# The projections of a differential-attention layer on one Trainium2 core: seven half-size block products over all 16 k-tiles instead of over 8, with weight sums made by accumulating transfers

## What is computed

```python
proj = u @ w_in                         # 512x2048 @ 2048x8192: q | k | v | z
logits = q_h @ k_h.T * scale + rel_bias # causal, 16 heads of width 128
p = softmax(logits)                     # heads 2i and 2i+1 make one pair
a = p[:, :, 0] - lam * p[:, :, 1]
o = rms_norm(a @ v_pair, subln_g) * (1 - lam_init)
y = (o * silu(z)) @ w_out               # 512x2048 @ 2048x2048
h = layer_norm(alpha * u + y, g, b)
```

## Time and profile before

| | |
|---|---|
| median of 3 runs | 921.08 us (920.71 to 921.26) |
| profiled execution, span from first to last instruction | 918.4 us |
| around the span (median less span) | 2.7 us |
| PE busy | 912.0 us, 99% of the span |
| DVE busy | 609.1 us, 66% |
| ACT busy | 381.8 us, 42% |
| POOL busy | 178.6 us, 19% |
| DMA | 124.53 MB, 136 GB/s on average |
| granted TensorE clock | 1.000 |

### The profile page before, as it was taken

How to read it: one execution, slowest core, us unless ns; L and a number is a source line. 1 busy time by engine, 2 the same in 40 slices (tenths; PEclk the granted TensorE clock), 3 DMA queues, 4 the chain that set the end, 5 groups by cost and what they waited for, 6 DMA issues and landing times.

```text
span 918.4 us, 14283 instructions
## 1 busy us (share of the span) xinstructions
PE 912.0 (99%) x5210; PEld 807.3 (88%) x5210; DVE 609.1 (66%) x1020; ACT 381.8 (42%) x653; POOL 178.6 (19%) x364
## 2 busy tenths in 40 slices
PE   9999999999999999999999999999999999999997
PEld 8888989898989898989898989898989888888886
DVE  5675857675767676767676767576757797434465
ACT  4443544444534354535453535353535454213211
POOL 1300313031303130313031303230322000000033
PEclk9999999999999999999999999999999999999999
DMA  8722506260625062606260625061606424443433
GB/s 308 288 94 97 181 32 198 85 188 23 206 74 188 25 204 78 193 26 197 90 190 26 200 80 188 23 206 46 189 26 217 191 92 160 183 149 99 154 116 114
DMA packets 43274, 124.53 MB, mean 136 GB/s; under 512 B 8160, under 2 KB 10208, under 8 KB 42992
## 3 DMA queue, kind: packets, MB, share of 16 engines
q1 hardware_dynamic: 29328, 97.27, 32.0%
q0 software_dynamic: 9504, 17.75, 6.2%
q10 hardware_dynamic: 4416, 9.18, 2.7%
HBM read 108.01 MB, written 13.15 MB: 132 GB/s over the span
## 4 chain that ended last, share of the span: by engine, by line
PE 99%; DMA 0%; DVE 0%; issue 0%; ACT 0%; SPq 0%; DVEq 0%; ACTq 0%
PE proj L1409 79%; PE att L1409 20%; DMA w_raw<-w_in_tiles_dram 0%; DVE big L1401 0%; DVE last_stats L1387 0%; ACT bias L900 0%; SPq L434 0%; DVE w_split L1250 0%; DVE mean_var L1390 0%; DVEq L1389 0%; ACTq L899 0%
## 5 line engine op out<-in xcount | busy, mean ns | idle before, releaser
L1409 PE MATMUL proj<-w_split,xg_split 128*128 128x512 f32 (+1 forms) x1512 | 294.5, 354 | 0.0
L1409 PEld LDWEIGHTS proj<-w_split,xg_split 128*128 128x128 f32 x1512 | 250.5, 189 | 39.9 <-issue 0.3
L1409 PE MATMUL proj<-xg_split,w_split 128*128 128x512 f32 (+1 forms) x1032 | 203.6, 355 | 0.3 <-DVE w_split L1250 0.3
L1409 PEld LDWEIGHTS proj<-xg_split,w_split 128*128 128x128 f32 x1032 | 171.8, 189 | 27.7 <-ACT xg_split L819 0.5
L920 DVE TENSOR_TENSOR w_split<-w_raw,w_split 128x1024 fp32r<-128x1024 f32 x98 | 119.9, 1224 | 93.6 <-ACT w_split L624 92.0
L624 ACT ACTIVATE w_split<-w_raw 128x1024 fp32r<-128x1024 f32 x98 | 103.7, 1058 | 135.5 <-PE proj L1409 128.5
L549 POOL DMA_DIRECT2D scratch<-scratch x224 | 110.7, 502 | 112.0 <-DVE scratch L1103 61.9
L1409 PE MATMUL att<-w_split,xg_split 128*128 128x512 f32 x432 | 99.9, 389 | 0.0
L1409 PEld LDWEIGHTS att<-w_split,xg_split 128*128 128x128 f32 x432 | 81.0, 188 | 16.8
L624 ACT ACTIVATE w_split<-x_res 128x1024 fp32r<-128x1024 f32 x42 | 44.6, 1061 | 106.0 <-PE proj L1409 67.2
L1409 PE MATMUL proj<-w_split,x_sums 128*128 128x256 f32 x672 | 82.9, 283 | 0.0
(11 more groups left out here) (153 smaller groups left out, 824.0 us busy)
## 6 DMA issues: line engine op xcount, KB each, us to landing
w_raw<-w_in_tiles_dram SPq DMA_DIRECT2D x112, 512.0 KB, 3.7
w_raw<-w_out_tiles_dram SPq DMA_DIRECT2D x32, 512.0 KB, 3.3
x_res<-w_in_tiles_dram SPq DMA_DIRECT2D x14, 512.0 KB, 3.9
bias_by_distance<-bias_lines POOLq DMA_DIRECT2D x8, 640.0 KB, 5.0
scratch<-scratch POOLq DMA_DIRECT2D x112, 40.0 KB, 3.1
bias<-bias_by_distance POOLq DMA_DIRECT2D x8, 512.0 KB, 4.0
x_res<-in_x_dram ACTq DMA_DIRECT2D x4, 1024.0 KB, 5.5
big<-x_cols_dram SPq DMA_DIRECT2D x7, 512.0 KB, 8.9
```

The lines of the kernel that those rows point to most:

```text
L1409: return nc.tensor.matmul(dst, lhsT, rhs, start=start, stop=stop, skip_group_check=True)
```

## The change

- Pairs 1 to 7 have 28 slots instead of 22: each phase is seven products in two blocks of 8 k-tiles (`BLOCKS = 2`), step by step: slot number = 14 x phase + 2 x step + block. Every slot is 24 matmuls with 256 moving columns. `plain_qk` and `plain_vz` go.
- The sums of x are now 8 (4 for each block). Their low parts take the place of x (`sums_low` in `big`), the high parts lie in a new buffer `x_extra` and in quarters of `xg_split` that are no longer read.
- Three of four sums of weights in each phase and block are made by a DMA of POOL that adds into the raw buffer (`add_block`, 128x1024 floats, `accum_op=ALU.add`), after the low part of the tile that lies there has been made. The fourth is still made by DVE (`w_sum_at`). The signs lie in the sums of x and in the final additions.
- The results are put together by DVE in pieces of 128x512 (`keep_sum`, `less_sum`, `finish_upper`, `finish_corner`, `finish_lower`).
- `operands` shrinks: v lies where q was. So v is moved only when the scores are made (`v_halves`), and q only when the last a times v of the pair before is done (`qk_head`).
- The attention of the pair before stands after slots 6 and 9, the scores after slots 18 and 21. The ring of descriptors of POOL's DMAs is half as large.

```diff
-PLAIN_K = 2 * SK
-PHASE = 11
+BLOCKS = KT // (2 * SK)
+PHASE = 7 * BLOCKS
 SLOTS = 2 * PHASE
...
+            def add_block(p, h, step):
+
+                for c in range(BLOCKS):
+                    i, block = RAW_OF[step] + c, ADD_AFTER[step]
+                    tile = QUARTERS + ((p - 1) * 2 + h) * 4 * BLOCKS + 4 * c + block
+                    pool.wait_ge(w_ready, slots_before(p) + h * PHASE + step * BLOCKS + c + 1)
+                    pool.dma_start(w_raw[:, i], w_in_tiles[tile * P:(tile + 1) * P, :], accum_op=ALU.add
+                                   ).then_inc(raw_added[i], 16)
...
                 if p + 1 < PAIRS:
                     load_bias(p + 1)
+                    add_block(p + 1, 0, 0)
                     pool.wait_ge(a_turned, p + 1)
                     swap_blocks(aT_blocks, 0, aT_done)
+                    add_block(p + 1, 0, 2)
+                    add_block(p + 1, 0, 3)
...
                 if p + 1 < PAIRS:
+                    add_block(p + 1, 1, 0)
                     pool.wait_ge(gated_turned, p + 1)
                     swap_blocks(gT, A_AT, nT_done)
+                    add_block(p + 1, 1, 2)
+                    add_block(p + 1, 1, 3)
...
+            def w_sum_at(p, j):
+
+                a = j + LEAD
+                p, a = (p, a) if a < SLOTS else (p + 1, a - SLOTS)
+                h, step, c = step_of(a)
+                if step == 1:
+                    wait_pair_raw(dve, p, h * PHASE + 3 * BLOCKS + c)
+                    nc.vector.tensor_tensor(w_raw[:, RAW_OF[2] + c], w_raw[:, RAW_OF[2] + c], w_raw[:, RAW_OF[3] + c],
+                                            ALU.add).then_inc(t_ready, 1)
...
+                if c == 0:
+                    if h == 0 and step == 0:
+                        pe.wait_ge(z_moved, 2 * p)
+                        pe.wait_ge(max_ready, p * (2 * ST) - 2)
+                    elif h == 0 and step == 1:
+                        pe.wait_ge(v_moved, 2 * p)
+                        pe.wait_ge(max_ready, p * (2 * ST))
+                    elif step < 2:
+                        pe.wait_ge(q_moved, 2 * p + step + 1)
...
-                    if j % PHASE < 7:
-                        product(p, j)
-                    elif j < PHASE:
-                        plain_qk(p, j)
-                    else:
-                        plain_vz(p, j)
+                    product(p, j)
                     inserts(p, j)
```

More of the change, by code:

```diff
@@ L346, in out_raw @@
         def out_raw(n):
-            return OUT_RAW[(n - TOTAL) % RING]
+            return (n - TOTAL) % RING
         def out_raw_count(n):
[L351 to L361, removed]
+            phases = 2 * (PAIRS - 1)
@@ L702, in exps, with v_halves @@
+            def v_halves(p):
+                act.wait_ge(scores_done, p * ST + ST)
+                act.wait_ge(lower_done, phase_number(p, 1) + 1)
+                for g in range(2):
+                    nc.scalar.activation(v[:, 0, g::2], half_banks(1, 0)[:, g], ACT.Copy).then_inc(v_hi, 1)
             def exps(p, t):
@@ L1211, in slot @@
[L1211 to L1225 removed]
+                    finish_lower(p, 0)
@@ new lines, in slot @@
+                if j == 11:
+                    qk_head(p, 1)
+                if last_pair(p):
+                    if j == SCORE_SLOTS[-1]:
+                        turn_last_a(False)
+                elif j == SCORE_SLOTS[-1] + 2:
+                    turn_a(p)
+                if j == SLOTS - 2:
+                    z_halves(p)
+                    if last_pair(p):
+                        g_early_lo(0)
+                if not (last_pair(p) and j + LEAD >= SLOTS):
+                    w_sum_at(p, j)
@@ L1295, in _ @@
                     dve.wait_ge(lam_step, 2)
-            vz_tiles(0)
+            first_vz(0)
+            combine(0, ST - 1)
+            turn_a(0)
+            for s in range(1, ST):
+                first_vz(s)
             with dve.Fori(1, PAIRS - 1) as p:
@@ L1299, in _ @@
                     slot(p, j)
-                vz_tiles(p)
-            for j in range(SLOTS - 1):
+                finish_lower(p, 1)
+                v_halves(p)
+            for j in range(SLOTS):
                 slot(PAIRS - 1, j)
-            vz_tile(PAIRS - 1, 0)
-            vz_tile(PAIRS - 1, 1)
-            slot(PAIRS - 1, SLOTS - 1)
-            vz_tile(PAIRS - 1, 2)
-            vz_tile(PAIRS - 1, 3)
-            g_early_lo(1)
+            finish_lower(PAIRS - 1, 1)
+            v_halves(PAIRS - 1)
             aT_split(PAIRS - 1, 0)
             aT_split(PAIRS - 1, 1)
-            combine(PAIRS - 1, 3)
+            g_early_lo(1)
             turn_last_a(True)
```

641 lines of the change are left out of this document (300 added, 341 removed).

## The result

The changed kernel takes **969.56 us** (median of 4 runs, 967.33 to 971.74) against 920.89 us (920.66 to 921.26) of the kernel before in the same session: 1.0529 times as long, 95% interval 1.051 to 1.0549. The forecast was 903.0 us, with a range that ended at 922. It is on the wrong side.

A forecast was written before the change was run, and what follows sets the result against it. The prediction took PE's matmuls as the bound: 918.4 us profiled plus 2.7 around it, less 22.9 of matmul work, gave 898.2; 4.9 us of waits for adding transfers made 903.1, said as 903, range 896.7 to 922.

The forecast's parts named there:

- Matmul term: PE's products: 336 half-width matmuls come and 192 full-width go, -3.27 us a pair, -22.9 us in seven pairs.
- X: Time of one adding transfer from POOL's issue to landing: taken as 5.5 us, bounds 4.0 to 8.0.
- a second read without the fixed part: Reasoning for 5.5 us: an add also fetches the buffer's 512 KB, about 1.4 to 1.5 us on a 4.0 us load.
- the adding transfer is slow: Rival: chain waits reach 22.9 us at a 6.65 us landing; 948 us at 8 us; chance 0.17.
- 7 x 0.7 + 0 + 0 = 4.9 us: Sum of PE's waits at 5.5 us landing: 0.7 seven times before slot 16, none before slots 2 and 7.
- adds behind swaps or loads: Sign of a wrong prediction: adds queue behind these, so a wait stands where no chain ends.
- chain C: a before slot 7: PE waits for landing time less 6.2 us, seven times; 0 at 5.5 us.
- Chain B: v before slot 2 of the next pair: PE waits for landing time less 5.5 us, six times; 0 at 5.5.
- Chain A: Head 0's q before slot 16: PE waits for landing time less 4.8 us, 0.7 us in each of seven pairs.
- POOL's swaps: 16 swaps (7.94 us) lie behind the adds and before their next need, with 3 us or more to spare.
- DVE isn't the bound: Rival: DVE becomes the bound between slots 19 and 25, 21.0 us against PE's 19.8; 905 us; chance 0.04.
- the half-width matmuls: Rival: in long rows they cost more than 0.1199 us, 0.1297 to break even, weight loads not hidden; chance 0.01.

The follow-up runs named there:

- e2: Changed kernel with no adding transfers issued and no waits for them, so three of four weight sums are not made: 904.51 us.
- e8: e2 with the last pair's 16 transposes of a spread four a slot, as in e5: 902.41 us, span 900.2 us.
- e11: Changed kernel without the four adding transfers a pair after step 3 and the wait for them in step 4: 917.63 us.
- e5: Changed kernel with the last pair's 16 transposes of a issued four a slot in slots 24 to 27 instead of all in slot 23: 970.03 us.
- e1: Changed kernel with POOL's transfers loading plainly into the same buffers instead of adding: 906.41 us.

## Why the prediction was wrong

- **Matmul term, -3.27 us a pair: right.** 87.73 us measured in e2 against 87.7. In e8, 898.2 us forecast without waits and 902.4 measured; the 4.2 us between are mostly 2.2 for g's split and 1.7 of clock behind it.
- **X = 5.5 for an adding transfer: right for one alone.** 5.1 to 5.7 us measured, and the bound "a second read without the fixed part" was the right reading of the earlier trace rows. This isn't the step that failed, though the rival "the adding transfer is slow" had its end.
- **The step that failed: "At X = 5.5: 7 x 0.7 + 0 + 0 = 4.9 us."** It gives one X to all three chains, as if each add had the DMA engines for itself. My own number said otherwise: two reads of 1.4 to 1.5 us each are some 2.8 us of all 16 engines, and four such come within 6 us. As a sign of being wrong I named adds behind swaps or loads, not adds behind each other. The change issues the non-urgent pair first. With the landing as it was, chain C is nearly right: 8.6 - 6.2 = 2.4 us in pair 3, and 2.8 were measured; in pairs 4 to 7 landings of 7.0 to 8.9 us give 0.8 to 2.7, and 1.2 to 3.0 were measured. For pairs 1 and 2 the row was worse (up to 11.4 and 9.6 us, waits of 6.9 and 4.2). The transfer of a row, not that of one add, was the number to put in. Together a cost 23.4 us where I had 0.
- **Chain B, v: the start was late, not the landing.** The add that v waits for landed in 5.2 us, so the formula gave no wait. But the row's 8.6 us at 356.11 held up ACT's and DVE's softmax work, which stands in order behind that split, and the split of tile 0 ended 14.3 us after the last scores (385.6 - 371.3) instead of 11.3. That is 3 us more, less a margin of 0.3: 2.7, and 2.1 were measured, six times. The chains are coupled; I had begun each at a point that I took from PE.
- **Chain A, q: about right**, 0.9 us a pair in the changed kernel against 0.7, with two errors that nearly cancel: the add landed in 5.3 us, not 5.5, and the formula, which gives 0.5 for that, was 0.4 us short. In e11 it's 1.2 at a landing of 5.6, 0.4 short again. I had the two adds issued 5.3 and 8.8 us after the start of slot 10; it was 5.8 and 9.4.
- **POOL's swaps "with 3 us or more to spare": right in the steady pairs, wrong in pair 1**, where the adds are issued only behind them.
- **The end of the last pair: not costed.** Its last slots are 2.88 us long where some were 5.45, and 16 transposes of 6.1 us in all stand in one of them. Waits of 2.4 and 4.4 us; e2 and e8 show 4.1 and 2.2 of it without any add. Spreading the transposes returns about 2 us without adds (e8 against e2) and nothing with them (e5).
- **The clock: not in the forecast.** About 14.6 us of the loss (17.1 by the windows, less 2.5 in which PE stood still anyway); e2's windows have 3.4 too.
- **Smaller misses.** DVE and ACT are 66% and 43% busy, not 70% and 47% (e2, whose waits are 7.0 us in all, has 71% and 47%).
- **The rivals.** "The adding transfer is slow" had the right side and, at X = 8, 948 us. I gave it 0.17 and looked for it in the single transfer's price. DVE isn't the bound (66%, and 71% in e2); neither are the half-width matmuls.

The sum against e8's span: 969.0 - 900.2 = 68.8 us. PE's waits are 56.5 us against 5.2, which is 51.3. PE's busy time is 908.9 us against 891.4, which is the other 17.5. Of these the clock takes 14.6 against 1.7, which is 12.9. The 4.6 us between fit an estimate: a lone 128x256 matmul is busy for 0.28 us (mean in the page of the kernel before), and in a row the next one starts after 0.12, so each of the 26 waits more leaves 0.16 us uncovered, 4.2 in all. That the clock's part follows from the waits rests on where the low windows stand, and on it going away in every kernel whose waits did; no run changed the one without the other.

## What to carry to other kernels

A transfer that is new to a kernel has two prices: how long it takes alone, and how long it keeps the DMA engines from the next one. Write down when each is issued; where several come within the time of one, the last of them is late by all those ahead, so the urgent ones have to be issued first and even then the row has a last. Where engines work in order, a late landing delays everything written behind it, so check the chains with each other's lateness, not each from an undisturbed start. And after a wait of a few microseconds PE may come back at a lower clock (here some 15 us over all), so a change that trades a little of its work for waits can pay more than the waits.

## What the runs showed of the hardware that I had not expected

- An adding transfer of 512 KB into a full buffer, issued by POOL: mostly 5.1 to 5.7 us alone, against 3.5 to 4.2 for a plain one in the same place (e1), and 2.8 us of all 16 DMA engines against 1.6. Its issue takes POOL longer too. One row of e1, then one of the changed kernel, for the 84 transfers (ns, minimum, median, maximum):

```profile
L602 POOL DMA_DIRECT2D w_raw<-w_in_tiles_dram x84: 530/541/617, 86.1 to 683.5; - x84
```

```profile
L602 POOL DMA_DIRECT2D w_raw<-w_in_tiles_dram x84: 838/852/1892, 85.9 to 744.4; - x84
```

- After PE's wait of 6.9 us the granted clock was 0.55 and 0.59 in two windows of 4 us. Shorter waits differ: those of 2.0 to 3.0 us that end at 300.9, 492.5, 511.7, 590.9 and 686.2 us are followed by a window at 0.57 to 0.69; those of 2.8 and 2.5 us before a in pairs 3 and 4 are not, and the clock stays at 1.0 from 308 to 492 us. The length of a wait alone doesn't tell which.
